# Routing tile by tile beside the output projection, and expert inputs gathered through an index table

## The reference, cut to what matters

```python
glog = xt @ w_group + b_group                 # 4 groups, the best one is taken
elog = (xt @ w_expert + b_expert)             # 32 experts, of the group's 8 the best two
ev, ei = lax.top_k(elog_g, 2)
ew = softmax(ev) * gw
order = argsort(e_flat)                       # 2048 (token, expert) pairs, sorted by expert
xin = x_pad[buf_tok].reshape(nblk, BLOCK, D)  # rows of an expert, in blocks
y = (silu(xb @ w1[e]) * (xb @ w3[e])) @ w2[e] # w1, w3: 1024 x 512; w2: 512 x 1024
out = segment_sum(y * buf_w, buf_tok)
```

## Time and profile before

| | |
|---|---|
| median of 3 executions | 1781.21 us |
| the profiled execution | 1784.23 us |
| its span, first to last instruction | 1782.4 us |
| PE, DVE, ACT, POOL busy in the span | 1557.8, 537.1, 348.3, 262.8 us |
| last product of the output projection ends | 1083.1 us |
| first expert matmul starts | 1152.1 us |
| last expert matmul ends | 1734.5 us |

### The profile page before, as it was taken

One profiled execution on the slowest core, in us unless ns is written; L12 is line 12 of the kernel. 1 busy time (PEld: TensorE's weight loads), 2 busy tenths in 40 slices (PEclk: granted clock), 3 DMA queues, 4 the chain that ended last, 5 costly groups with the idle time before them and its releaser, 6 DMA issues.

```text
span 1782.4 us, 20856 instructions
## 1 busy us (share of the span) xinstructions
PE 1557.8 (87%) x7526; PEld 828.0 (46%) x7527; DVE 537.1 (30%) x1378; ACT 348.3 (20%) x859; POOL 262.8 (15%) x363
## 2 busy tenths in 40 slices
PE   6999998989989898988999994199799999889990
PEld 3554543434444444443444552156355666446650
DVE  4210005665565545553222215011011111101116
ACT  3000003343433433342000111011011111111112
POOL 2000002333232232221000000300000000000003
PEclk9999999999999999998999997599899999999995
DMA  9124602443111111002536410979999999999967
GB/s 254 26 59 57 132 0 100 166 142 95 30 33 34 30 24 42 25 18 77 204 115 232 172 53 18 341 283 380 383 389 384 379 391 381 391 390 383 381 223 283
DMA packets 130215, 334.21 MB, mean 188 GB/s; under 512 B 36792, under 2 KB 72664, under 8 KB 120944
## 3 DMA queue, kind: packets, MB, share of 16 engines
q1 hardware_dynamic: 112208, 291.88, 46.8%
q0 software_dynamic: 9552, 29.55, 5.0%
q10 hardware_dynamic: 8400, 12.07, 1.9%
HBM read 276.06 MB, written 57.41 MB: 187 GB/s over the span
## 4 chain that ended last, share of the span: by engine, by line
PE 71%; DMA 9%; DVE 8%; SPq 6%; issue 3%; ACT 2%; POOL 2%; ACTq 0%; POOLq 0%; DVEq 0%
PE PS L741 13%; PE PS L642 10%; PE PS L531 10%; PE PS L755 7%; PE PS L704 6%; PE PS L673 5%; SPq L301 5%; PE PS L628 4%; PE PS L589 4%; PE PS L608 3%; PE PS L526 2%; DMA BA<-w 2%; DMA WA<-w 2%; DMA BA<-rows_d 2%; DVE mx L1022 1%
## 5 line engine op out<-in xcount | busy, mean ns | idle before, releaser
L642 PE MATMUL PS<-WA 128*128 128x512 f32 x512 | 260.3, 621 | 17.8 <-ACT WA L833 17.8
L741 PE MATMUL PS<-WA,BA 128*64 128x256 f32 x2048 | 235.8, 388 | 14.1 <-DMA WA<-w 12.9
L741 PEld LDWEIGHTS PS<-WA,BA 128*64 128x64 f32 x2048 | 172.9, 140 | 84.6 <-issue 22.1
L531 PE MATMUL PS<-WA,BA 128*128 128x512 f32 x416 | 183.1, 601 | 5.1 <-DVE WA L937 5.1
L1248 POOL TENSOR_SCALAR BA<-BA,rin,gates 128x640 f32<-128x640 f32 (+7 forms) x128 | 99.8, 780 | 301.8 <-DVE rin L1045 301.7
L1161 DVE SCALAR_TENSOR_TENSOR BA<-BA,PS 128x256 f32<-128x256 f32 x46 | 19.4, 421 | 408.4 <-ACT BA L880 408.4
L642 PEld LDWEIGHTS PS<-WA 128*128 128x128 f32 x512 | 85.6, 191 | 111.5 <-issue 80.9
L826 ACT ACTIVATE BA<-PS,ngm 128x640 f32<-128x640 f32 (+7 forms) x128 | 89.7, 701 | 218.2 <-DVE ngm L1023 218.0
L531 PEld LDWEIGHTS PS<-WA,BA 128*128 128x128 f32 x416 | 79.6, 193 | 103.9 <-issue 98.3
L755 PE MATMUL PS<-WA,BA 128*64 128x512 f32 x512 | 116.9, 597 | 11.7 <-DVE BA L1171 7.6
L1287 POOL DMA_DIRECT2D BA<-rows_d x92 | 48.1, 522 | 531.1 <-PE PS L722 528.1
(11 more groups left out here) (207 smaller groups left out, 1361.4 us busy)
## 6 DMA issues: line engine op xcount, KB each, us to landing
WA<-w SPq DMA_DIRECT2D x66, 2048.0 KB, 34.4
BA<-w SPq DMA_DIRECT2D x30, 2048.0 KB, 36.7
rows_d<-WA SPq DMA_DIRECT2D x7, 2048.0 KB, 7.5
BA<-rows_d POOLq DMA_DIRECT2D x94, 128.0 KB, 7.2
rows_d<-BA ACTq DMA_DIRECT2D x92, 128.0 KB, 7.8
WA<-w_in SPq DMA_DIRECT2D x16, 512.0 KB, 5.5
gates_d<-WA SPq DMA_DIRECT2D x32, 256.0 KB, 2.2
WA<-gates_d SPq DMA_DIRECT2D x8, 1024.0 KB, 6.0
```

What stands on the lines that cost most here:

```text
L531: mm = pe.matmul(PS[:, j % 4, :], ws[:, c % 6, k, :], hnT[:, k, 512 * h:512 * h + 512], start=(k == 0), stop=(k == KT - 1))
L642: mm = pe.matmul(PS[:, 6, :], gw[:, j, k, :], hnT[:, k, 512 * hf:512 * hf + 512], start=(k == 0), stop=(k == KT - 1))
L741: mm = pe.matmul(PS[DH * h:DH * h + DH, bank, 0:256], xT[:, k, :], w[par][:, k, 256 * h:256 * h + 256], start=(k == 0), stop=(k == KT - 1))
```

## The change

**Order of the projection.** PE now computes a tile's second half in two parts of four products, with the router's product of the tile before between them, and a small rank product (`rank`, two matmuls of 32 columns) for the tile two before.

**Routing by tile.** DVE no longer waits for all tiles. In the loop over tiles it now runs `place(i-2)`, `logits(i-1)` and `choose(i-1)` ahead of tile i's h2: 5, 1 and 16 small instructions. The row number of a pair is now known at once, as 1024 times the expert plus the rank so far, since each expert has its own region of 1024 entries. After the last tile DVE counts blocks as before, and raises `routed`; the values for the end of the program (`slots_i`, `tokw`) come behind that, as does a table of the first table row of every block (`block_row_i`), which one transpose turns into a row on one partition.

**Index table instead of scattered rows.** SP stores each tile's normed rows once, in token order, to `hn_d` (HBM, 2 KB half rows; 8 stores of 512 KB). POOL scatters 64-byte entries that name half rows into `ids_d` (16 indirect DMAs of 128 entries, two a tile); the table is zeroed early in the attention stage by one more DMA. The 16 scatters of rows are gone.

**Expert loop.** For every block POOL now waits for the block's indices and for `x_tr`, copies the indices, issues one indirect gather of 128 half rows from `hn_d` into `xin`, reads the next block's table row into a register, and issues two loads of 64 indices of 4 bytes each for the block after.

**SP.** Expert 2's weights are loaded when the last logits are there and all stores of h2 and hn have landed, no longer behind the scatter.

The diff, cut to its core:

```diff
-    rows_d = scratch("rows_d", ((MAXB + 1) * SLOTS, D))
+    rows_d = scratch("rows_d", (MAXB * SLOTS, D))
+    hn_d = scratch("hn_d", (2 * SEQ, D // 2))
+    ids_d = scratch("ids_d", ((NE + 1) * SEQ, ENTRY), I32)
...
+        ids_z = ids_d.rearrange("r n -> (r n)").rearrange("(p a n) -> p a n", p=P, n=128)
         rows_z = rows_d.rearrange("r n -> (r n)").rearrange("(p a n) -> p a n", p=P, n=512)
+        sp.dma_start(ids_z, zeros[:, 0:128].bitcast(I32).unsqueeze(1).to_broadcast([P, NE + 1, 128])) \
+            .then_inc(S["zero_done"], 16)
...
+        hn_rows = hn_d.rearrange("(t h) n -> t (h n)", h=2)
+
+        def store_normed(i):
+
+            sp.wait_ge(S["hn2_done"], i + 1)
+            sp.dma_start(hn_rows[P * i:P * i + P, :], mT[:, i, :, :].rearrange("p k n -> p (k n)")) \
+                .then_inc(S["hn_st"], 16)
...
+                store_normed(i - 1)
         sp.wait_ge(S["h2_done"], TT)
         sp.dma_start(h2_d[SEQ - P:SEQ, :], h2[:, (TT - 1) % 2, :]).then_inc(S[f"h2_st{(TT - 1) % 2}"], 16)
-
-        sp.wait_ge(S["scattered"], 16 * 2 * TT)
+        store_normed(TT - 1)
+
+        sp.wait_ge(S["log_done"], TT)
+        sp.wait_ge(S["hn_st"], 16 * TT)
...
-        for i in range(TT + 1):
-            if i < TT:
-                if i >= 2:
-                    pe.wait_ge(S["h2_done"], i - 1)
-                for n in range(2):
-                    for k in range(KT):
-                        mm = pe.matmul(PS[:, 2 * (i % 2) + n, :], mT[:, i, k, :], wout[:, k, 512 * n:512 * n + 512],
-                                       start=(k == 0), stop=(k == KT - 1))
-                    if n == 0 and i >= 1:
-                        turn_normed(i - 1)
-                mm.then_inc(S["out_ps"], 1)
-            else:
+        def rank(i):
+            pe.wait_ge(S["assigned"], i + 1)
+            if i >= 1:
+                pe.wait_ge(S["slotx_done"], i)
+            pe.matmul(PS[:, 7, 0:NE], tri[:, :], assign[:, NE * i:NE * i + NE], start=True, stop=True)
+            pe.matmul(PS[:, 7, NE:2 * NE], ones[:, :], assign[:, NE * i:NE * i + NE], start=True, stop=True) \
+                .then_inc(S["route_ps"], 1)
+
+        def project(i, n, ks):
+            for k in ks:
+                mm = pe.matmul(PS[:, 2 * (i % 2) + n, :], mT[:, i, k, :], wout[:, k, 512 * n:512 * n + 512],
+                               start=(k == 0), stop=(k == KT - 1))
+            return mm
+
+        for i in range(TT):
+            if i >= 2:
+                pe.wait_ge(S["h2_done"], i - 1)
+            project(i, 0, range(KT))
+            if i >= 1:
                 turn_normed(i - 1)
+            if i >= 2:
+                rank(i - 2)
+            project(i, 1, range(KT // 2))
             if i >= 1:
                 router(i - 1)
-
-
-        pe.wait_ge(S["assigned"], 1)
-        pe.matmul(PS[:, 0, 0:256], tri[:, :], assign[:, :], start=True, stop=True)
-        pe.matmul(PS[:, 1, 0:256], ones[:, :], assign[:, :], start=True, stop=True).then_inc(S["route_ps"], 1)
+            project(i, 1, range(KT // 2, KT)).then_inc(S["out_ps"], 1)
+        turn_normed(TT - 1)
+        rank(TT - 2)
+        router(TT - 1)
+        rank(TT - 1)
...
+        pe.sem_inc(S["x_tr"], 1)
+        pe.wait_ge(S["row_col"], 1)
+        pe.transpose(PS[0:1, 6, 0:P], block_row, ident[:, :]).then_inc(S["row_ps"], 1)
         pe.wait_ge(S["routed"], 1)
-        pe.wait_ge(S["x_blk"], 32)
+        pe.wait_ge(S["x_blk"], 16)
...
-                rows_in = pe.snap(b * 32 + 64)
+                rows_in = pe.snap(b * 16 + 32)
...
-            act.wait_ge(S["x_tr"], b + 2)
+            act.wait_ge(S["x_tr"], b + 3)
...
+        def first_of_max(out, src, best, b, rev):
+
+            step(dve.tensor_reduce(best, src, X, ALU.max))
+            step(dve.scalar_tensor_tensor(b, src, best, rev, ALU.is_equal, ALU.mult))
+            step(dve.tensor_reduce(c1, b, X, ALU.max))
+            return dve.tensor_scalar(out, b, c1, None, ALU.is_equal)
...
+        def choose(m):
+
+            dve.wait_ge(S["log_done"], m + 1)
+            groups4, experts = lgs[:, m, 0:NG], lgs[:, m, NG:NG + NE]
+            step(first_of_max(oh4, groups4, top[:, 0, m:m + 1], b4, rev4))
+            step(dve.tensor_scalar(m4, oh4, -NEG, NEG, ALU.mult, ALU.add))
+            step(dve.tensor_tensor(open32.rearrange("p (g e) -> p g e", g=NG), experts.rearrange("p (g e) -> p g e", g=NG),
+                                   m4.unsqueeze(2).to_broadcast([P, NG, EPG]), ALU.add))
+            step(first_of_max(onehot[:, m, 0, :], open32, top[:, 1, m:m + 1], b32, rev32))
+            step(dve.scalar_tensor_tensor(rest32, onehot[:, m, 0, :], 2 * NEG, open32, ALU.mult, ALU.add))
+            step(first_of_max(onehot[:, m, 1, :], rest32, top[:, 2, m:m + 1], b32, rev32))
+            dve.tensor_tensor(assign[:, NE * m:NE * m + NE], onehot[:, m, 0, :], onehot[:, m, 1, :], ALU.add) \
+                .then_inc(S["assigned"], 1)
+
+        def place(m):
+
+            dve.wait_ge(S["route_ps"], m + 1)
+            step(dve.tensor_tensor(row32, next_row, PS[:, 7, 0:NE], ALU.add))
+            step(dve.tensor_tensor(next_row, next_row, PS[:, 7, NE:2 * NE], ALU.add))
+            step(dve.tensor_tensor(pick, onehot[:, m, :, :], row32.unsqueeze(1).to_broadcast([P, 2, NE]), ALU.mult))
+            step(dve.tensor_reduce(slot_f[:, m, :], pick, X, ALU.add))
+            dve.tensor_copy(slotx_i[:, m, :], slot_f[:, m, :]).then_inc(S["slotx_done"], 1)
...
+            if i >= 2:
+                place(i - 2)
+            if i >= 1:
+                logits(i - 1)
+                choose(i - 1)
...
-            if i >= 1:
-                logits(i - 1)
-
-
-        def first_of_max(src, scores_out, best, rev, a, b, c):
...
+        place(TT - 1)
+
+        dve.wait_ge(S["tables"], 3)
+        step(dve.tensor_tensor(cnt, next_row, first_row, ALU.subtract))
...
-        step(dve.tensor_scalar(base32, starts_f[:, 0:NE], float(SLOTS), None, ALU.mult))
-        step(dve.tensor_tensor(offs[:, :, :], offs[:, :, :], base32.unsqueeze(1).to_broadcast([P, TT, NE]), ALU.add))
-        step(dve.tensor_tensor(offs[:, :, :], offs[:, :, :], PS[:, 0, 0:256].rearrange("p (t n) -> p t n", t=TT), ALU.add))
-        for c in range(2):
-            step(dve.tensor_tensor(G32[1], onehot[c], offs[:, :, :], ALU.mult))
-            step(dve.tensor_reduce(G8[8 + c], G32[1], X, ALU.add))
-            step(dve.tensor_copy(slots_i[:, c, :], G8[8 + c]))
         dve.sem_inc(S["routed"], 1)
+
+        step(dve.tensor_tensor(G4[3][:, :, :], lgs[:, :, 0:NG], top[:, 0, :].unsqueeze(2).to_broadcast([P, TT, NG]), ALU.subtract))
+        dve.tensor_tensor(G8[4], top[:, 2, :], top[:, 1, :], ALU.subtract).then_inc(S["route_arg"], 1)
+        step(dve.scalar_tensor_tensor(reach, starts_f[:, 0:NE], -float(SLOTS), first_row, ALU.mult, ALU.add))
+        step(dve.scalar_tensor_tensor(reach, starts_f[:, 0:NE], number, reach, ALU.is_le, ALU.mult))
+        step(dve.tensor_reduce(far, reach, X, ALU.max))
+        dve.scalar_tensor_tensor(block_row, number, float(SLOTS), far, ALU.mult, ALU.add).then_inc(S["row_col"], 1)
+        dve.wait_ge(S["row_ps"], 1)
+        dve.tensor_copy(block_row_i, PS[0:1, 6, 0:P]).then_inc(S["row_tab"], 1)
...
+        g.iota(entry, [[2 * P, TT], [1, ENTRY]], base=0, channel_multiplier=2).then_inc(S["tables"], 1)
+        pool.wait_ge(S["tables"], 1)
+
+        def scatter_ids(i):
+
+            pool.wait_ge(S["slotx_done"], i + 1)
+            for c in range(2):
+                g.indirect_dma_start(ids_d[:, :], bass.IndirectOffsetOnAxis(ap=slotx_i[:, i, c:c + 1], axis=0),
+                                     entry[:, i, :], None).then_inc(S["scattered"], 16)
+
+        pool.wait_ge(S["zero_done"], 16 * (ZPARTS + 1))
+        for i in range(TT - 2):
+            scatter_ids(i)
...
+        for i in range(TT - 2, TT):
+            scatter_ids(i)
+        pool.wait_ge(S["scattered"], 16 * 2 * TT)
+        pool.wait_ge(S["hn_st"], 16 * TT)
+        pool.wait_ge(S["h2T_ps"], TT)
         pool.wait_ge(S["routed"], 1)
-        pool.wait_ge(S["zero_done"], 16 * ZPARTS)
-        pool.wait_ge(S["hn2_done"], TT)
-        for i in range(TT):
-            for c in range(2):
-                g.indirect_dma_start(rows_d[0:MAXB * SLOTS, :], bass.IndirectOffsetOnAxis(ap=slots_i[:, c, i:i + 1], axis=0),
-                                     mT[:, i, :, :].rearrange("p k n -> p (k n)"), None).then_inc(S["scattered"], 16)
-        pool.wait_ge(S["scattered"], 16 * 2 * TT)
-
-
+
+        def load_ids(row):
+
+            for n in range(2):
+                pool.dma_start(ids[SLOTS * n:SLOTS * n + SLOTS, 0:1], ids_d[bass.ds(row, SLOTS), n:n + 1],
+                               allow_slow_non_contiguous=True).then_inc(S["ids_in"], 16)
+
+        load_ids(0)
         total = pool.value_load(starts_i[0:1, NE:NE + 1], min_val=NE, max_val=MAXB)
-        for n in range(2):
```

(39 more changed lines are left out.)

65 lines of the change are left out of this document (32 added, 33 removed).

## The result

| | before | changed |
|---|---|---|
| median of the runs | 1778.41 us (1777.58, 1778.41, 1781.21; a fourth, of 9073.13, is left out) | 1727.62 us (1727.31 to 1730.02, 4 runs) |
| profiled execution | 1784.23 us | 1727.31 us |

The ratio is 0.971, 95% interval 0.970 to 0.973: **2.9% faster**. The forecast was 1778 us with a range of 1752 to 1852 and a chance of 0.04 for faster. In the experiments' runs, before has a median of 1778.2 to 1779.2 us.

A forecast was written before the change was run, and what follows sets the result against it. The loop was taken as limited from two sides, PE and full DMA engines, with PE idle about 60 us ahead of it. 1784.2 - 24 (earlier start) + 18 (POOL's cycle) = 1778.2 us, forecast 1778, range 1752 to 1852.

The forecast's parts named there:

- Part 1: Start of the loop: projection's last product to first expert matmul takes 45.0 us against 69.0, 24 us earlier (17 to 31).
- Rival (c): At the loop's start: slow `choose` or crawling scatters and index loads; gain under 10 us, about 1792 to 1802; chance 0.08.
- Part 2: Expert loop: POOL's longer cycle of reads and index loads makes it about 600 us against 582.5, +18 us (0 to 124).
- the stream needs 553 us: Expert loop: loading expert weights and moving the blocks' data takes 553 us at 385 GB/s, resting 8% of the time.
- the 39 us that it put down to weights: Expert loop before: 582.5 us against 543 us for 46 blocks of 11.81 us; the excess was called weight cost.
- POOL's cycle: Expert loop: from one block's indices landing to the next's, 14.5 us heavy, 10.3 light, mean 13.1, 1.3 over PE's.
- (a): Expert loop: index loads are hidden and the cycle stays near 10.5 us, under PE's 11.8; 1760 us, chance 0.24.
- (b): Expert loop's gather: two half rows do not share a packet, so 128 + 16 packets; 1854 us, chance 0.28.
- The waits at `turn_rows`: Sign in the expert loop: PE waits there for `xin`, 1 to 2 us a block, and less for weights.
- The clock: Feared in the loop: clock falls in new short waits; 0.93 to 0.95 over the whole loop would add 20 us.

The follow-up runs named there:

- the one read: Kernel before, with a block's rows read by one plain DMA of 128 partitions instead of two of 64; 1746.8 us, ratio 0.983.

## Why the prediction was wrong

**Part 1, right in mechanism, sized a little short.** Forecast -24 us (bounds 17 to 31), measured 30.7 - 2.6 = 28.1. The projection's end came 2.6 us later, not 3.0. The landings were taken as 7.5, 7.5 and 3.1 us and were 6.1, 3.8 and 3.4. The reason given, expert 2's traffic, is real, as the two runs with a later load show, but the load ended at about 1111 us, while the index loads, issued from 1107.55 us on, were under way; they landed at 1111.9. The start alone is worth 27.7 us in time (the run with the old reads). Rival (c) is out.

**Part 2, the step that failed:** "the stream needs 553 us (30 experts of 6.3 MB and 46 blocks of 0.52 MB at 385 GB/s)". I read the 383 to 395 GB/s of the earlier trace rows as what the engines can do, since their share was full, and carried them over to a kernel with other reads. They were what two 64-partition reads left of 407 to 409 (the changed kernel and the one read, in the windows of the table above, where before has 385). A full share says that packets are in flight all the time, not that they go at full speed; in the block looked at above the weights are slow in the 4 us in which the reads run and fast behind them, and the rows of a few microseconds that I did have the earlier trace rows were not set against each other by MB per share. So the sum had no term for the loop's largest effect: 35 us of stream by the estimate, 24 of loop as measured. And of the 39 us that it put down to weights only 26.2 were waits for them; 8.7 more of them went as PE's own busy time.

**The size of POOL's cycle failed too.** The sum took 10.0 us until both reads have landed (0.6 + 9.4) and 3.0 us for the index loads behind them. But 9.4 us was one of the slow landings: the median over the loop was 7.3 us for a read of before, and is 8.0 for the gather and 7.7 for an index load. In the block shown above the gather lands after 8.0 us, and the index loads, issued 1.1 us behind it, after 8.6, so about 2 us later than the gather. A cycle that the indices end behind a punctual one is 12.0 to 13.2 us instead of 14.5 (one, with the late gather, 15.2). That the halves had made the 10.0 us is not shown: with the gather in halves such cycles take 12.8 to 13.8 us, with an issue of some 1.3 us more in each. The count was right: 3600 packets of POOL's queue in 25 blocks (1270 to 1570 us) are 144 a block. Since the cycle fits under PE's 11.8 us in 36 of 46 blocks, the index loads cost next to nothing: leaving all of them out gave 1 to 3 us over the whole loop, where +18 was forecast.

**Rivals.** (a), hidden index loads, 1760 us, was the right mechanism for POOL, yet it too kept all 39 us of weight waits; the measured time of the profiled execution is (a) less the loop's 24 us, 4 for a start better than forecast, and the 5 of scatter ahead of the projection. (b) is out: of the 3600 packets 1600 are the large ones, and carry 6.57 MB, so 4 KB each and 64 a block, two half rows in each. The waits at `turn_rows`, 1 to 2 us a block by the forecast, were 1.4 us in the whole loop.

**The clock** went the other way than feared: with fewer waits the granted clock is 0.99 instead of 0.98 over the loop, and PE's busy time is 8.7 us less for as many matmuls.

**Does it add up?** The start alone -27.7, the wide read alone -31.4, together -59.1, against -50.8 in the changed kernel. Of the 8.3 missing, 3.3 are the first index load (38.3 us to the first expert matmul against 35.0 with the old reads, which need no indices), and 4.1 the loop (558.8 against 554.7), of which 3.3 go with the index loads. The rest, 1 us, is within the runs' scatter.

## What to carry to other kernels

A full DMA share is no bound: divide the share by the megabytes of the big stream, with and without each small transfer beside it, before a rate is carried over to a changed kernel. A small transfer into on-chip memory is to cover all 128 partitions, even at the price of another row order; here that one edit was worth 1.7%, as much as a reworked routing stage. When a change swaps one kind of transfer for another, its shape is a part of the change and needs its own line in the sum.

## What the runs showed of the hardware that was not expected

- Reads into 64 or 32 partitions raise the price of another queue's packets: a 16 KB packet of weights takes 0.82 to 0.85 us beside them, 0.62 to 0.63 beside reads into 128 partitions, 0.61 alone; over the loop, weights cost 41 to 42 engine-us per MB instead of 38 to 39. Stores out of 64 partitions don't (38.8 and 38.7; 0.61 us).
- An indirect gather of 2 KB rows packs two of them in a packet (64 packets of 4 KB for a block's 128 half rows), as a plain read does.
- Index loads of 4 bytes a row land in 1.8 us with idle engines and 8.6 us beside weights; they hardly slow the weights (two a block make the loop 3 us longer).
- Moving a 6 MB load from beside two small DMAs to beside the third moved the wait with it: 3.1 and 1.9 us gained, 5.1 lost (the first of the two later loads).
